# Delta rule in two groups of steps, six ticks apart, with two projections between the products of the last step

## The chip, the core and the metric

The program runs on one core of a Trainium2 chip. Times are device microseconds of one execution; lower is better. In the profile PE is TensorE's matmuls and PEld its weight loads, DVE is VectorE, ACT is ScalarE, POOL is GpSimd, and SP is SyncE, which only starts transfers. The text calls VectorE "Vector".

## What is computed

The reference runs two blocks of a network on 256 tokens of width 1024, in float32. The first has attention, a gated recurrence, a dense MLP and a mixture of 8 experts. The second has a linear attention in two forms, the gated delta rule and HGRN2, each run in both directions over 256 context and 256 latent tokens, then a mixture of 32 experts. This case is about the delta rule and what stands right behind it. The reference computes, for each direction, chunk by chunk of tokens:

```python
a = jnp.where(strict, jnp.einsum('nbhik,nbhjk->nbhij', kb, k) * decay, 0.0)
rhs = jnp.concatenate([v * beta[..., None], kb * jnp.exp(gcum)[..., None]], axis=-1)
sol = lax.linalg.triangular_solve(a, rhs, left_side=True, lower=True, unit_diagonal=True)
u, w = sol[..., :dv], sol[..., dv:]

def step(s, inp):
    qc, kc, uc, wc, gc, dc = inp
    v_new = uc - jnp.einsum('bhck,bhkv->bhcv', wc, s)
    g_last = gc[..., -1]
    s_new = s * jnp.exp(g_last)[..., None, None] + jnp.einsum(
        'bhck,bhcv->bhkv', kc * jnp.exp(g_last[..., None] - gc)[..., None], v_new)
    ...
    o = jnp.einsum('bhck,bhkv->bhcv', qc * jnp.exp(gc)[..., None], s) + jnp.einsum(
        'bhij,bhjv->bhiv', jnp.einsum('bhik,bhjk->bhij', qc, kc) * dc, v_new)
    return s_new, o
```

Only the state `s` goes from one chunk to the next. The triangular solve and all of `a` belong to one chunk alone.

## The kernel before

Everything is laid out by hand: five instruction streams, one per engine, that meet only in semaphores. Each engine works through its stream in order. `pe.wait_ge(*at("gram", n))` waits until the n-th event of that name has been counted.

**The delta rule.** The tokens are cut into four chunks of 128, two of context, two of latent tokens; `TILE` gives the order for each direction `d`. The loop `for s_ in range(4)` stands once in each of the four compute streams. One step does both directions, four heads each, so most operations are four matmuls of 128x128, or one vector operation of 128x512. Its phases are:

1. Gram (L1037, L1039): `k k^T` and the cumulated gates, in steps 2 and 3 also `k q^T` (L1043). Vector and ScalarE form decays from it (L1673 to L1677, L1884).
2. Start: Vector forms `A` (L1683), masks it and subtracts it from the identity, which gives `T` (L1690, L1691); in steps 2 and 3 it also masks `attT` (L1687, L1688). TensorE transposes `A` (L1051), ScalarE copies it to `At`, and Vector forms `U` from that (L1695, L1696).
3. Six levels that invert the triangle by doubling. GpSimd masks `At` for each level (L2204). TensorE multiplies that with `T` (L1066, the product), ScalarE copies the result to `P1`, TensorE multiplies `P1` with `U` in two ways (L1073 for T, L1075 for U, the level step), and Vector subtracts both from `T` and `U` (L1702, L1703). The sixth level has no T.
4. Key: GpSimd scales `v` and `k` by the gates (L2210, L2212, L2216; L2215 for q), TensorE multiplies the key by `U` (L1083), and ScalarE copies it as `nw`.
5. Value: the new value from `U`, `vb`, `nw` and the state `Sd` (L601), which Vector copies as `vn` (L1706).
6. State: in steps 2 and 3 the output (L601), and the addition to the state (L1103), which Vector adds in (L1720, L1721; event `S_ready`).

The steps do not overlap: the gram product of a step waits for `S_ready` of the step before. All eight PSUM banks serve one step, four per direction, and its nine work buffers per direction, `WK[d]`, lie in the arena:

```python
WK = [[area(8192 + 4608 * d + 512 * i, H, P) for i in range(9)] for d in range(2)]
...
if s_:
    pe.wait_ge(*at("S_ready", n - 1))
```

**Behind it** stand two projections of the second linear attention, `zd` and `hq` (helper line L601, four chains of eight products each, 64 matmuls in the trace), a sum of squares between them (L1114, event `o_ss`), ScalarE's Ln and Exp of it (`rs_done`), the SiLU of hq (`hq_ready`), then the projections `f0` and `hi`. `f0` waits for `hq_ready`.

**The weights.** A ring of six slots of 2 MB holds weights; SP loads them in the order of a list (`plan`, `plan2`: k, v, q, zd, hq, f0, hi, f1, hz, gd0, gd1, gh0, gh1, ...), each when the slot's former user has been read. `READ` names that event, and SP's queue is in order.

**The start of the kernel.** TensorE waits for 19 small rows, transposes them to columns (L832, L833), and then transposes the normed input (`norm_T(0)`, L632). On ScalarE `norm(0)` stands behind the exponentials for lambda and the SiLU of c; on Vector it stands behind the same work (L1437 to L1447).

The functions that the change touches, with the lines of the profile:

## Time and profile before

| What | us |
|---|---|
| Median of 3 runs | 2853.5 (2852.21 to 2855.32) |
| The profiled execution | 2852.58 |
| Its span, first to last instruction | 2850.8 |
| TensorE busy in the span | 2497.5 (88%) |
| Vector busy | 630.4 (22%) |
| ScalarE busy | 369.2 (13%) |
| GpSimd busy | 151.4 (5%) |
| Delta rule, first gram to last state product | 1652.1 to 1941.9 |
| First f0 matmul | 1978.1 |

The span is what lies between the first and the last instruction of the profiled execution; the time of a run is 1.8 us longer. In time by stretch each line gives a stretch, its length, the busy time of each engine with the number of instructions, the granted TensorE clock as a share of full speed, and the share and rate of the transfers. A float32 matmul shows as two instructions, so that four of 128x128 are "x8". Busy times of TensorE overlap a little, since matmuls are pipelined; what a group costs is read from one start to the next, or from the chain.

### The profile page before, as it was taken

The numbers are of one execution on the slowest core, as the hardware profiler recorded it, in microseconds if no ns is written. First come the engines' busy times: TensorE is split into PE (matmuls) and PEld (weight loads), VectorE is DVE, ScalarE is ACT, GpSimd is POOL, SyncE is SP. The second block draws the span as 40 slices with busy tenths as digits, with TensorE's granted clock in tenths as the row PEclk, the third lists the DMA queues.
The fourth block names the chain that finished last, engine by engine and source line by source line (L and its number), as shares of the span: only waits on it lengthen the run. The fifth ranks groups of instructions, "written<-read, shape, count | busy, mean of one in ns | idle before, by whom it ended". The sixth has DMA issues, their size and how long they took to land.

```text
span 2850.8 us, 52823 instructions
## 1 busy us (share of the span) xinstructions
PE 2497.5 (88%) x24386; PEld 1612.6 (57%) x24386; DVE 630.4 (22%) x1191; ACT 369.2 (13%) x595; POOL 151.4 (5%) x140
## 2 busy tenths in 40 slices
PE   5768997699999999999998967678898959999896
PEld 4536775556656555655656667676467634444343
DVE  1441001300000000000002344551534142222223
ACT  1021001100000000000001221111323011011101
POOL 1000000000000000000000023321201000000000
PEclk9879999799999999999999988888999979999998
DMA  7484333399989989998996200001111249999994
GB/s 280 148 296 147 120 133 126 125 393 353 393 312 352 394 309 393 352 394 315 353 393 228 89 1 1 1 1 60 59 60 59 89 177 399 404 397 398 401 401 186
DMA packets 273245, 676.25 MB, mean 237 GB/s; under 512 B 5876, under 2 KB 9423, under 8 KB 268815
## 3 DMA queue, kind: packets, MB, share of 16 engines
q1 hardware_dynamic: 270608, 666.91, 62.3%
q0 software_dynamic: 2112, 6.04, 0.6%
q8 instruction: 184, 3.01, 0.4%
q14 instruction: 23, 0.18, 0.0%
q10 hardware_dynamic: 318, 0.10, 0.0%
HBM read 671.98 MB, written 1.05 MB: 236 GB/s over the span
## 4 chain that ended last, share of the span: by engine, by line
PE 59%; DMA 10%; DVE 5%; ACT 3%; POOL 3%; issue 2%; SPq 2%; DVEq 0%; POOLq 0%; ACTq 0%
PE ps L691 21%; PE ps L601 14%; PE ps L712 10%; DMA ring<-in_w_exp_up 10%; PE ps L776 5%; ACT arena L1884 2%; SPq L548 2%; PE ps L1075 1%; PE ps L1073 1%; PE ps L1066 1%; PE ps L698 1%; PE ps L674 1%; POOL arena L2236 1%; ACT L1884 1%; POOL arena L2204 1%
## 5 line engine op out<-in xcount | busy, mean ns | idle before, releaser
L691 PE MATMUL ps<-ring,arena 128*32 128x256 f32 x10752 | 598.0, 382 | 16.6 <-issue 15.3
L691 PEld LDWEIGHTS ps<-ring,arena 128*32 128x32 f32 x10752 | 349.0, 111 | 249.6 <-issue 32.0
L601 PE MATMUL ps<-hT,ring 128*128 128x256 f32 (+1 forms) x1792 | 444.2, 409 | 19.6 <-ACT arena L1884 7.3
L1884 ACT ACTIVATE arena<-ps 128x512 f32<-128x512 f32 (+4 forms) x347 | 186.8, 556 | 1960.7 <-PE ps L691 576.1
L601 PEld LDWEIGHTS ps<-hT,ring 128*128 128x128 f32 x1792 | 346.9, 194 | 122.6 <-issue 69.4
L712 PE MATMUL ps<-ring,arena 128*32 128x256 f32 x5376 | 300.5, 379 | 0.0
L776 PE MATMUL ps<-ring,arena 128*64 128x512 f32 x1024 | 233.8, 611 | 29.4 <-DMA ring<-in_w_exp_up 26.5
L712 PEld LDWEIGHTS ps<-ring,arena 128*32 128x32 f32 x5376 | 173.9, 110 | 115.3 <-issue 1.3
L1359 DVE TENSOR_TENSOR arena<-arena,ps 128x384 f32<-128x384 f32 x56 | 31.0, 554 | 825.2 <-ACT arena L1884 825.2
L776 PEld LDWEIGHTS ps<-ring,arena 128*64 128x64 f32 x1024 | 81.1, 141 | 178.9 <-issue 178.9
L601 PE MATMUL ps<-arena 128*128 128x128 f32 (+1 forms) x1144 | 146.1, 290 | 20.6 <-DVE arena L1387 7.5
L601 PEld LDWEIGHTS ps<-arena 128*128 128x128 f32 x1144 | 142.8, 206 | 22.5 <-DVE arena L1387 7.7
L2204 POOL TENSOR_TENSOR arena<-arena,table 128x512 f32<-128x512 f32 x48 | 65.3, 1367 | 1533.6 <-ACT arena L1884 1476.3
L792 PE MATMUL ps<-ring,arena 128*64 128x512 f32 x512 | 113.4, 595 | 0.0
L1884 ACT ACT_TABLE_LOAD x64 | 82.1, 1283 | 193.1 <-PE ps L601 87.0
L1066 PE MATMUL ps<-arena 128*128 128x128 f32 x384 | 59.4, 305 | 34.0 <-POOL arena L2204 20.7
L1884 ACT ACTIVATE arena<-arena 128x512 f32<-128x512 f32 (+3 forms) x78 | 63.1, 845 | 186.9 <-DVE arena L1677 41.1
L941 PE MATMUL ps<-ring,arena 128*128 128x512 f32 x176 | 79.0, 592 | 0.0
L1410 DVE TENSOR_TENSOR arena<-arena,ps 128x512 f32<-128x512 f32 x16 | 11.0, 687 | 300.0 <-PE ps L776 300.0
L1066 PEld LDWEIGHTS ps<-arena 128*128 128x128 f32 x384 | 52.9, 214 | 39.2 <-POOL arena L2204 22.5
L792 PEld LDWEIGHTS ps<-ring,arena 128*64 128x64 f32 x512 | 35.3, 137 | 66.6 <-issue 66.6
L601 PE MATMUL ps<-ring,arena 128*128 128x512 f32 (+1 forms) x160 | 58.1, 524 | 12.3 <-DVE arena L1265 9.7
(319 smaller groups left out, 1721.5 us busy)
## 6 DMA issues: line engine op xcount, KB each, us to landing
ring<-in_moe_wg SPq DMA_DIRECT2D x56, 2048.0 KB, 11.3
ring<-in_moe_wu SPq DMA_DIRECT2D x56, 2048.0 KB, 16.4
ring<-in_moe_wd SPq DMA_DIRECT2D x56, 2048.0 KB, 17.2
ring<-in_w_exp_gate SPq DMA_DIRECT2D x32, 2048.0 KB, 17.5
ring<-in_w_exp_up SPq DMA_DIRECT2D x32, 2048.0 KB, 18.8
ring<-in_w_exp_down SPq DMA_DIRECT2D x32, 2048.0 KB, 14.8
ring<-in_w_in SPq DMA_DIRECT2D x13, 2048.0 KB, 8.9
ring<-in_w_ada SPq DMA_DIRECT2D x12, 2048.0 KB, 8.1
```

Source lines behind the costliest of these rows:

```text
L548: sp.dma_start(dst, w[2 * p + j, :, :].rearrange(rows_, p=P))\
L601: last = mm(outp, l, r, start=(i == 0), stop=(i == n - 1))
L674: last = mm(ps[:, 4 + q, t * S:(t + 1) * S], un_GcT[32 * q:32 * q + 32, 1 - b, 3 * t + r, :], ysb[32 * q:32 * q + 32, r * S:(r + 1) * S], ...
L691: last = mm(flat[32 * q:32 * q + 32, S * r:S * r + S], x_[:, k, 32 * r:32 * r + 32], gu[:, :, k, q * P:(q + 1) * P], start=(k == 0), stop= ...
L712: last = mm(flat[32 * q:32 * q + 32, 3 * 512 + S * r:3 * 512 + S * r + S], un_actT[:, c, r, :], d_[:, c, q * S:(q + 1) * S], start=(j == 0 ...
L776: last = mm(ps[64 * j:64 * j + 64, part, :], x_[:, k, 64 * j:64 * j + 64], weights(3 * j + part, KC)[:, k, :], start=(k == 0), stop=(k == ...
L792: last = mm(ps[64 * j:64 * j + 64, 4 + h_, :], pr_actT[:, c, 64 * j:64 * j + 64], weights(3 * j + 2, 4)[:, c, h_ * 512:(h_ + 1) * 512], st ...
L941: last = mm(ps[:, 4 + 2 * t + c, :], actb[:, (n - 1) % 4, t * P:(t + 1) * P], d_[:, j, c * 512:(c + 1) * 512], start=(n == 1), stop=(n == ...
L1066: last = mm(ps[:, 4 * d + 1, h * P:(h + 1) * P], Ao[:, h, :], T[:, h, :], start=True, stop=True)
L1359: V.tensor_tensor(un_act, un_sg, up_, ALU.mult).then_inc(inc("m1_act"), 1)
L1884: return nc.scalar.activation(*a, **k)
L2204: G.tensor_tensor(WK[d][2 + l % 2], WK[d][1], rep(level_mask(l, d == 0), 4), ALU.mult)\
```

## The change

It has three parts.

1. The steps of the delta rule are put into two groups, even and odd. Time is counted in 30 ticks; step `s_` starts in tick 6 `s_` (`FIRST`) and has twelve phases, one per tick: gram, turn, start of U, six levels, key, value, state. So from tick 6 to tick 23 each tick holds one level of one step and another phase of the other. Each stream has a loop over ticks. TensorE does the level products, then the other phase, then the level steps. Each group has four PSUM banks, two per direction, its own work buffers and its own semaphores for T, U, P and the masks; a product now waits for T alone. The buffers of group 1 lie in ring slots 0 to 2, so the slots of k, v and q are only given back with the last `S_ready`. `k q^T` moves from gram to key. GpSimd's scalings are spread over the levels.
2. `zd` and `hq` are computed in ticks 27 to 29, chain by chain between the products of step 3. The sum of squares moves to banks 4 and 5, hq to 2 and 3; `f0` waits for `rs_done` and `hi` for `hq_ready`.
3. At the start of the kernel `norm(0)` comes first on ScalarE and Vector, and `norm_T(0)` comes before the transposes of the rows.

```diff
-        READ = {"k": ("k_proj", 4), "v": ("v2_proj", 4), "q": ("q_proj", 1), "zd": ("zd_proj", 1), "hq": ("hq_proj", 1),
+        READ = {"k": ("S_ready", 8), "v": ("S_ready", 8), "q": ("S_ready", 8), "zd": ("zd_proj", 1), "hq": ("hq_proj", 1),
...
-        WK = [[area(8192 + 4608 * d + 512 * i, H, P) for i in range(9)] for d in range(2)]
+        spare = ring[:, 0:3, :].rearrange("p s n -> p (s n)")
+
+        def work(g, o):
+            return area(8192 + o, H, P) if g == 0 else spare[:, o:o + 512].rearrange("p (a b) -> p a b", a=H)
+
+        WK = [[[work(g, 4608 * d + 512 * i) for i in range(9)] for d in range(2)] for g in range(2)]
...
+        FIRST = (0, 6, 12, 18)
+        GRAM, INV, HALF, UPDATE, KEY, VALUE, STATE = 0, 1, 2, 8, 9, 10, 11
+
+        def in_tick(k):
+            return [(s_, k - FIRST[s_]) for s_ in range(4) if GRAM <= k - FIRST[s_] <= STATE]
+
+        def levels(k):
+            return [(s_, p - HALF) for s_, p in in_tick(k) if HALF < p <= UPDATE]
```

TensorE's stream, with the helpers that wait:

```diff
+            def turn(s_, d):
+                n = 2 * s_ + d
+                A, (bx, by) = WK[s_ % 2][d][0], banks(s_, d)
+                pe.wait_ge(*at("A_ready", n + 1))
+                pe.wait_ge(*at("eR", n + 1))
...
+            def product(s_, d, l):
+                g = s_ % 2
+                Ao, T, (bx, by) = WK[g][d][2 + l % 2], WK[g][d][4], banks(s_, d)
+                pe.wait_ge(*at("Aoff%d_ready" % g, level_count(s_, d, l)))
+                pe.wait_ge(*at("T%d_ready" % g, t_count(s_, d, l - 1)))
+                if l == 1:
+                    pe.wait_ge(*at("U%d_ready" % g, u_count(s_, d, 0)))
...
+            def step(s_, d, l):
...
+                pe.wait_ge(*at("P%d_copied" % g, level_count(s_, d, l)))
+                pe.wait_ge(*at("U%d_ready" % g, u_count(s_, d, l - 1)))
...
+            for k in range(FIRST[3] + STATE + 1):
+                for s_, l in levels(k):
                     for d in range(2):
...
+                        product(s_, d, l)
+                for s_, p in in_tick(k):
                     for d in range(2):
...
+                        if p == GRAM:
+                            gram(s_, d)
+                        elif p == KEY:
+                            key(s_, d)
+                        elif p == VALUE:
+                            value(s_, d)
+                        elif p == STATE:
+                            state(s_, d)
+                if k == FIRST[3] + KEY:
+                    pe.wait_ge(*at("S_ready", 6))
+                    for m in range(3):
+                        project("zd", m, 0)
+                elif k == FIRST[3] + VALUE:
+                    project("zd", 3, 0)
+                    for m in range(2):
+                        project("hq", m, 2)
+                elif k == FIRST[3] + STATE:
+                    for m in range(2, 4):
+                        project("hq", m, 2)
+                for s_, l in levels(k):
+                    for d in range(2):
+                        step(s_, d, l)
+                for s_, p in in_tick(k):
+                    if p == INV:
+                        for d in range(2):
+                            turn(s_, d)
...
-                    pe.wait_ge(*at("hq_ready", 1))
+                    pe.wait_ge(*at("rs_done", 1))
```

Vector's loop and GpSimd's (ScalarE's has the copies of P1 first, then gram, turn or key):

```diff
+            for k in range(FIRST[3] + STATE + 1):
+                for s_, p in in_tick(k):
+                    for d in range(2):
+                        if p == GRAM:
+                            gram(s_, d)
+                        elif p == INV:
+                            start_T(s_, d)
+                        elif p == HALF:
+                            start_U(s_, d)
+                        elif p == KEY and s_ >= 2:
+                            attend(s_, d)
+                        elif p == VALUE:
+                            value(s_, d)
+                        elif p == STATE:
+                            state(s_, d)
+                for s_, l in levels(k):
+                    for d in range(2):
+                        step(s_, d, l)
...
+                        if l <= 4:
+                            offs(s_, d, l + 2)
+                for s_, p in in_tick(k):
+                    for l in (1, 2):
+                        for d in range(2):
+                            if p == HALF:
+                                offs(s_, d, l)
+                    for d in range(2):
+                        if p == HALF + 1:
+                            key_decayed(s_, d)
+                        elif p == HALF + 5:
+                            key_to_end(s_, d)
+                        elif p == HALF + 6:
+                            value_scaled(s_, d)
```

The start, on TensorE and on ScalarE:

```diff
             pe.wait_ge(*at("table_in", 16))
+            norm_T(0)
             pe.wait_ge(*at("rows_in", 16 * (len(ROWS_A) + len(ROWS_B))))
...
-
-            norm_T(0)
...
+            norm(0, res, ("x_in", 16))
             ac.wait_ge(*at("cols_ready", 1))
...
-            norm(0, res, ("x_in", 16))
```

TensorE at the end of the levels of step 0, before the change (L1066 product, L1075 the U product, L1083 key):

```order
L1066 MATMUL ps<-arena 128x128 [waits TU_ready,Aoff_ready]
L1066 MATMUL ps<-arena 128x128 x3
L1066 MATMUL ps<-arena 128x128 [waits TU_ready,Aoff_ready]
L1066 MATMUL ps<-arena 128x128 x3
L1075 MATMUL ps<-arena 128x128 [waits P1_copied]
L1075 MATMUL ps<-arena 128x128 x3
L1075 MATMUL ps<-arena 128x128 [waits P1_copied]
L1075 MATMUL ps<-arena 128x128 x3
L1083 MATMUL ps<-arena 128x128 [waits kbg_ready,TU_ready]
L1083 MATMUL ps<-arena 128x128 x3
L1083 MATMUL ps<-arena 128x128 [waits kbg_ready,TU_ready]
L1083 MATMUL ps<-arena 128x128 x3
```

The same place after the change (L1086 the U product, L1074 product, L1095 key; names with 0 and 1 belong to the groups):

```order
L1086 MATMUL ps<-arena 128x128 [waits U0_ready,P0_copied]
L1086 MATMUL ps<-arena 128x128 x3
L1086 MATMUL ps<-arena 128x128 [waits U0_ready,P0_copied]
L1086 MATMUL ps<-arena 128x128 x3
L1074 MATMUL ps<-ring 128x128 [waits U1_ready,T1_ready,Aoff1_ready]
L1074 MATMUL ps<-ring 128x128 x3
L1074 MATMUL ps<-ring 128x128 [waits U1_ready,T1_ready,Aoff1_ready]
L1074 MATMUL ps<-ring 128x128 x3
L1095 MATMUL ps<-arena 128x128 [waits ops_ready,U0_ready]
L1095 MATMUL ps<-arena 128x128 x3
L1095 MATMUL ps<-arena 128x128 [waits ops_ready,U0_ready]
L1095 MATMUL ps<-arena 128x128 x3
```

The first level product of step 1, in the ring's buffers, now stands between the last level step of step 0 and its key product. Before, it stood behind key, value and state of step 0 and gram and turn of step 1.

ScalarE at the start of the kernel, before (rows of `pA`, `pB`, `rowsA` and `rowsB` are lambda, the gates and c; `res` is the input):

```order
L1884 ACT_TABLE_LOAD [waits ve_mixer1]
L1884 ACTIVATE small<-small 128x2 [waits ve_mixer1]
L1884 ACTIVATE small<-pA 128x4 [waits ac_mixer1]
L1884 ACTIVATE small<-small 128x4 [waits ac_step]
L1884 ACT_TABLE_LOAD
L1884 ACTIVATE small<-small 128x4 [waits ac_step]
L1884 ACT_TABLE_LOAD [waits scT_zero]
L1884 ACTIVATE rowsA<-pB 128x4 [waits ac_mixer1]
L1884 ACTIVATE rowsA<-pB 128x4
L1884 ACTIVATE rowsB<-pB 128x4 x2
L1884 ACTIVATE arena,small<-res 128x1024 [waits x_in,ac_mixer1]
L1884 ACTIVATE arena,small<-res 128x1024
```

After:

```order
L1964 ACT_TABLE_LOAD
L1964 ACTIVATE arena,small<-res 128x1024 [waits x_in]
L1964 ACTIVATE arena,small<-res 128x1024
L1964 ACT_TABLE_LOAD [waits ms_ready]
L1964 ACTIVATE small<-small 128x2 [waits sumsq]
L1964 ACT_TABLE_LOAD
L1964 ACTIVATE small<-small 128x2 [waits ac_step]
L1964 ACTIVATE small<-small 128x2 [waits ve_mixer1,rstd_ready]
L1964 ACTIVATE small<-pA 128x4 [waits ac_mixer1]
L1964 ACTIVATE small<-small 128x4 [waits ac_step]
L1964 ACT_TABLE_LOAD
L1964 ACTIVATE small<-small 128x4 [waits ac_step]
```

The squares of the input moved from behind that work to the head, behind a table load that waits for nothing.

## Rows read from the trace of the kernel before

**Rows 1.** Time by stretch: busy us (count) of each engine, granted clock, DMA
```profile
core 0: us, PE busy (x) PEld busy (x) DVE busy (x) ACT busy (x) POOL busy (x), PEclk, DMA share, GB/s
1652.10:1719.00 66.90, 50.61 (x361) 47.91 (x361) 29.94 (x47) 12.33 (x24) 22.16 (x18) 0.83 0.00 1
...
1863.60:1941.90 78.30, 55.94 (x425) 53.67 (x423) 36.91 (x58) 13.37 (x26) 25.01 (x20) 0.83 0.00 1
1669.20:1677.60 8.40, 8.03 (x48) 7.76 (x49) 3.57 (x4) 1.19 (x2) 3.63 (x3) 0.67 0.00 0
1669.20:1707.20 38.00, 34.40 (x272) 33.22 (x272) 15.82 (x23) 7.16 (x12) 12.05 (x10) 0.93 0.00 1
```
**Rows 2.** In order of time (start us, us, what): one level; its chain
```profile
1679.32 1.13 PE L1066 MATMUL ps<-arena 128*128 128x128 f32 x8 [0.65 <-DVE arena L1703]
...
1682.35 0.69 DVE L1702 TENSOR_TENSOR arena<-arena,ps 128x512 f32<-128x512 f32 x1 [3.17 <-PE ps L1075]
...
1685.57 1.13 PE L1066 MATMUL ps<-arena 128*128 128x128 f32 x8 [0.65 <-DVE arena L1703]
...
1680.45 0.89 PE ps L1073 x8
```
**Rows 3.** In order of time, opening of step 0; in brackets idle before and releaser
```profile
1652.14 2.08 PE L1037 MATMUL ps<-arena 128*128 128x128 f32 x8 [6.25 <-DVE arena L1662]
...
1659.94 1.12 DVE L1683 SCALAR_TENSOR_TENSOR arena<-ps,small,arena 128x128 f32<-128x128 f32 x4
...
1661.10 0.69 DVE L1690 TENSOR_TENSOR arena<-arena,table 128x512 f32<-128x512 f32 x1
...
1669.20 2.05 PE L1066 MATMUL ps<-arena 128*128 128x128 f32 x8 [4.35 <-POOL arena L2204]
```
**Rows 4.** The same after the last level of step 0; then clock by stretch there
```profile
1709.58 1.13 PE L1083 MATMUL ps<-arena 128*128 128x128 f32 x8 [2.26 <-POOL arena L2216]
...
1712.00:1714.00 2.00, 1.30 (x6) 1.33 (x7) 0.00 (x0) 0.00 (x0) 0.56 (x1) 0.56 0.00 0
1714.00:1716.00 2.00, 2.00 (x13) 2.00 (x13) 0.00 (x0) 0.60 (x1) 0.00 (x0) 0.59 0.00 0
```
**Rows 5.** In order of time, end of delta rule to f0; clock of its start
```profile
1961.43 13.98 PE L601 MATMUL ps<-hT,ring 128*128 128x256 f32 x64
...
1966.02 1.06 ACT L1884 ACTIVATE arena<-arena 128x1024 f32<-128x1024 f32 x1
...
1978.13 1.71 PE L601 MATMUL ps<-hT,ring 128*128 128x512 f32 x2 [2.72 <-ACT arena L1884]
...
1978.00:1980.00 2.00, 1.87 (x3) 0.97 (x4) 0.00 (x0) 0.00 (x0) 0.00 (x0) 0.62 1.05 409
```
**Rows 6.** Loads, KB each, us to landing; waits of TensorE for DMA, whole span
```profile
ring<-in_w_in SPq DMA_DIRECT2D x13, 2048.0 KB, 8.9
...
table<-in_k_table POOLq DMA_DIRECT2D x1, 1216.0 KB, 12.5
res<-in_x POOLq DMA_DIRECT2D x1, 1024.0 KB, 9.4
...
PE ps L776 <- DMA ring<-in_w_exp_up: 26.5, 14, 2.6
```
**Rows 7.** In order of time, the opening of the kernel
```profile
24.91 1.06 ACT L1884 ACTIVATE arena<-res 128x1024 f32<-128x1024 f32 x1
...
32.04 3.68 PE L632 MATMUL ps<-table,arena 128*128 128x128 f32 x16 [13.93 <-DVE arena L1265]
...
36.50 27.89 PE L601 MATMUL ps<-hT,ring 128*128 128x256 f32 x128 [0.78 <-DVE hT L1271]
```
**Rows 8.** In order of time, Vector beside GpSimd in step 1 and later
```profile
1729.88 6.45 POOL L2204 TENSOR_TENSOR arena<-arena,table 128x512 f32<-128x512 f32 x4 [1.72 <-ACT arena L1884]
1730.19 1.63 DVE L1696 TENSOR_TENSOR arena<-table,arena 128x512 f32<-128x512 f32 x1
...
2052.14 1.33 DVE L1779 COPY_PREDICATED arena<-table,ps 128x512 f32<-128x512 int32 x2
```

More of the change, by code:

```diff
@@ L1107, in _ @@
             pe.wait_ge(*at("S_ready", 8))
[L1108 to L1111 removed]
             pe.wait_ge(*at("o_sq", 1))
             for i in range(2):
[L1114 removed]
+                last = mm(ps[:, 4 + i, :], ones, rs[:, 2 * i:2 * i + 2, :], start=True, stop=True)
```

394 lines of the change are left out of this document (200 added, 194 removed).

## The prediction

> **What bounds the kernel now.** I read the page first, then time by stretch, then the chain and the instructions in order of time of one stretch, then the waits at its two ends. The profiled execution took 2852.6 us (span 2850.8), 0.9 us under the median of the three runs, 2853.5; the sum below is made against 2852.6. TensorE is busy 88% of the span and leads the chain; expert weights end the last 500 us. Neither is touched. The change sits in two places: the first 36.5 us, and the delta rule with the two projections behind it.
>
> The delta rule runs from 1652.1 to 1941.9 in four steps, the first of 66.9 and the last of 78.3 us, and TensorE is busy only 51 and 56 us of these, at a granted clock of 0.83 [rows 1]. Inside a step one level takes 6.25 us (1679.32 to 1685.57): two products and the T and U products of both directions are six groups of four matmuls (x8 in the rows) at 0.89 us, so 5.4 us of work, and 0.65 us go in waiting for the second of Vector's subtractions [rows 2]. So the levels are nearly full; the loss is around them. Step 0 needs 17.06 us from its first gram product to the first level product (1652.14 to 1669.20) [rows 2, 3], its six levels 38.0 us [rows 1], and the rest of the 66.9 is the tail, in which TensorE waits for GpSimd's scaled operands (2.26 us before the first key product) and then runs at 0.56 to 0.59 of the clock until 1716 [rows 4]. Outside the levels a step thus costs 66.9 - 38.0 = 28.9 us, and 78.3 - 38.0 = 40.3 us in the last two, which also form an output.
>
> **The change, part by part.** Call u the time of four matmuls of 128x128 at full clock, 0.89 us [rows 2]. The new order has 30 ticks. In ticks 6 to 23 one step is in its levels 4 to 6, key, value and state, while the next one is in gram, turn, start and levels 1 to 3. The order of the matmuls is in the listings: between the level products and the level steps of one group now stands a phase of the other.
>
> (1) Opening of step 0 to its first level product: unchanged, 17.1 us. (2) Levels 1 to 3 of step 0 alone: the first as now, 8.4 us (1669.2 to 1677.6, at a clock of 0.67 [rows 1]); the other two lose the 0.65 us wait, since a product now waits for T only, not for T and U: 5.6 us each. Sum 19.6.
>
> (3) Ticks 6 to 23, counted in u. By tick of a group of six: level 4 with gram 6 + 4; level 5 with turn 6 + 1; level 6 has no T product, 4; level 1 with key 6 + 2; level 2 with value 6 + 4; level 3 with state 6 + 2. That is 47u when step 1 is the older one; 45u when it is step 0 (its value has no old state, 2u less); 53u when it is step 2 (kq +2, output +4). Together 145u = 129.1 us. To this come waits that the order leaves. In the tick with turn, Vector has 2 x (1.12 + 0.69 + 0.69) = 5.0 us of start-T before 2.75 us of level subtractions (four at 0.69) [rows 2, 3], against 6.2 us of TensorE work: about 1.6 us late. In the next tick TensorE has 4u = 3.6 us, but the first product of the younger step needs the At copy, GpSimd's two masks and Vector's start-U; TensorE waited 4.35 us there [rows 3], and more for the second direction, which comes 2.4 us later. Against 3.6 us of cover I take 2.9 us late. So 4.5 us per group, 13.5 in all. After such a gap the clock falls: after the wait before 1709.58 the stretch 1712 to 1716 got 0.56 to 0.59 [rows 4], which costs about 2 us; three gaps, 6 us. Sum (3): 148.6 us, 8.3 us per tick.
>
> (4) Ticks 24 to 29, step 3's last levels, key, value, state: 6 + 6 + 4 + 4 + 4 + 6 = 30u = 26.7 us, with 0.6 us of waits left, and six of the eight projection chains between them. Both projections have 64 matmuls; at 13.98 us for one [rows 5] a chain costs 3.5 us, six cost 21.0. The copies of nw and vn and the masks of attT (0.6 to 1.4 us each) hide beneath them; without that cover each would show. Sum 48.3.
>
> (5) From the last state product to the first f0 product. Now: 1941.9 to 1978.1, 36.2 us [rows 5]. After: two chains (7.0 us) cover Vector's last S (about 2.4 us after the product) and ScalarE's square; then o_ss 1.9 us, Ln and Exp 1.1 each with a table load of 1.3 between: 12.5 us with handovers [rows 5]. f0 now waits for that Exp (rs_done) and no longer for the SiLU of hq, which moves beneath f0's 29.4 us. The idle of 3.6 us before f0 replaces one of 2.7 us, after which f0 already began at 0.62 of the clock [rows 5]: no difference.
>
> Sum: 17.1 + 19.6 + 148.6 + 48.3 + 12.5 = 246.1 us against 1978.1 - 1652.1 = 326.0. Gain 79.9.
>
> (6) The ring. Group 1 works in slots 0 to 2, so hi, f1 and hz, loaded behind the k, v and q projections so far, are asked for only after the last S, and on SP's queue gd0, gd1 and gh0 stand behind them. A 2 MB load of w_in lands in 8.9 us [rows 6]; hi is first needed about 10 + 29.4 us after the last S, f1 much later. Cost 0, hidden under f0; without f0 in its slot hi would cost up to 8.9 us.
>
> (7) The start. The norm stood on ScalarE behind lam and the c gates: its square began at 24.91, the first projection at 36.50 [rows 7]. The input lands 9.4 us after its issue at 1.3, so at 10.7, the table 12.5 us after 2.1 [rows 6]. Squares, Ln, Exp and the scaling take 24.91 to 32.04, 7.1 us: 17.8 [rows 7]. The 19 small rows are in at 17.5, where the transposes of rows stand now. Sixteen transposes 3.7, the two transposes of rows 0.55, Vector's four ops 0.6, four hT copies 2.9, which no longer run beneath the transposes, and 0.5 of handovers: 26.0. Gain 10.5; the 3.9 us without TensorE before the projection cost about 2 of it, by what the clock does behind such gaps [rows 4, 5]. Gain 8.5. The weights of win0 were issued at 0.74 and are no later than the table. ScalarE's lam and c work moves beneath the first projection (27.9 us); until then nothing waits for it. Of the waits of TensorE for loads the large one is that for w_exp_up in the last stage, 26.5 us in 14 [rows 6]; nothing before it hangs on a weight, so the shift should be kept.
>
> Total gain 79.9 + 8.5 = 88.4, and 2852.6 - 88.4 = **2764 us**. Bounds: with no waits and no clock losses (13.5 + 6 + 2 less) 2743; with the lock below in full 2795.
>
> **The lock between Vector and GpSimd.** A Vector operation with both inputs in SBUF took 0.69 us alone [rows 3] and 1.63 us while four of GpSimd's masks ran, 1.61 us each; two COPY_PREDICATED with one input in PSUM took 1.33 together beside a GpSimd operation [rows 8]. The level subtractions read one operand from PSUM, so I take 0.68 for them beside GpSimd too. The Trainium skill (SBUF — State Buffer, Who interferes with whom) says that Vector with two SBUF inputs and a GpSimd operation that reads SBUF exclude each other for a whole instruction, and that one SBUF input is free of it; the trace agrees, 1.63 against 0.66. By that rule the start, gram, attT and S operations, which now meet the masks of the other group, would all pay, and the sum would be the first rival's.
>
> **Rivals.** *The lock bounds the ticks.* Some 15.5 locked Vector operations per step (gram 2 to 4, start-T 4, start-U 4, attT 2, S 2, rounded), each 0.94 us longer: 14.6 us per step. If they all lie on the path in the three groups, 43.8 us in place of my 13.5: 2764 + 30.3 = 2795. For it: both queues are in order, and Vector does the other group's phase before the level's subtractions. Against: GpSimd is busy only 22 us of 67 and 25 of 78 per step [rows 1], and level ticks have 2.5 us of it.
> *The ticks run in series.* If the phases overlap nothing, a tick costs 6.25 plus a sixth of 28.9 to 40.3, mean 5.8: 18 x 12.0 = 216 us in place of 148.6: 2831. For it: one semaphore waited for in a wrong place holds a whole in-order queue. Against: products and steps of a level are independent of the phase between them.
> *Slower.* Series and full lock together: 216 + 43.8 in place of 148.6, so 2875. It decides in ticks 6 to 23, where all other parts sum to 97.5, from a tick of (326.0 + 8.5 - 97.5) / 18 = 13.2 us on; I expect 8.3.
> *The start gives nothing*, because something other than the norm holds the first projection: 2773.
>
> **Chances.** Forecast 0.77, lock 0.14, series 0.05, slower 0.02, no gain at the start 0.02. The range is 2740 to 2798: forecast with its bounds, the lock, and the start without gain; outside stay series and slower. 0.2% is 5.7 us, about what a measurement of this kernel tells from no change. Faster by more 0.97, within 0.01, slower 0.02.
>
> **What would show it.** First projection at about 26 us. Delta rule from its first gram to f0 in 246 us, the clock in it above 0.93 instead of 0.84, level ticks of 7 to 10 us, and TensorE's waits at the first product of steps 1 to 3 near 3 us. Locked: Vector's start operations at 1.6 us mean. Series: TensorE busy 50 of 70 us as now. hi loads begin after the last S and no matmul waits for them. I am wrong if a double tick averages over 10 us or if the second half does not simply move earlier.

## The result, and the profile after

The changed kernel took 2768.4 us, median of four runs (2762.65 to 2773.21), beside 2853.3 us of the kernel before on the same chip: a ratio of 0.970, with a 95% interval of 0.968 to 0.972. Five more runs later gave a median of 2764.0 (2762.19 to 2769.42). The prediction was 2764. The profiled execution took 2765.3 us, span 2763.4.

From the first gram product to the first f0 matmul, "the stretch" from here on, TensorE now needs 244.2 us in place of 326.0. Time by stretch in the changed kernel, first the opening with levels 1 to 3 of step 0, then the first and the last of the three groups of six ticks, and the whole:

```profile
core 0: us, PE busy (x) PEld busy (x) DVE busy (x) ACT busy (x) POOL busy (x), PEclk, DMA share, GB/s
1643.69:1680.28 36.59, 27.86 (x184) 26.35 (x185) 19.99 (x32) 7.32 (x16) 15.41 (x12) 0.74 0.00 0
1680.28:1725.06 44.78, 42.04 (x362) 40.78 (x361) 30.15 (x48) 11.99 (x24) 21.68 (x18) 1.00 0.01 1
...
1772.27:1825.79 53.52, 49.37 (x427) 48.01 (x425) 38.60 (x59) 12.99 (x26) 25.07 (x20) 1.00 0.01 1
1643.69:1887.90 244.21, 220.11 (x1717) 209.81 (x1717) 137.53 (x215) 58.10 (x107) 98.02 (x84) 0.96 0.05 17
```

And the whole stretch in the kernel before:

```profile
1652.14:1978.13 325.99, 244.02 (x1716) 229.11 (x1717) 139.24 (x221) 62.20 (x113) 99.08 (x84) 0.85 0.03 8
```

TensorE's busy time fell from 244.0 to 220.1 us, for the same matmuls (1716 and 1717 records) at a granted clock of 0.96 in place of 0.85, and what is not busy fell from 82.0 to 24.1 us. So of 81.8 us, 57.9 are idle time that went and 23.9 are clock. In [rows 1] one step of 66.9 us had 51 us of work at 0.83; now six ticks of 44.8 us hold 42.0 at 1.00.

TensorE's largest waits in the stretch for Vector (us in total, times, longest):

```profile
PE ps L1074 <- DVE arena L1747: 6.9, 3, 4.3
...
PE ps L1063 <- DVE arena L1736: 4.0, 2, 2.5
PE ps L1074 <- DVE ring L1747: 3.5, 3, 2.2
PE ps L1074 <- DVE arena L1754: 3.2, 3, 1.4
PE ps L1074 <- DVE ring L1754: 1.2, 1, 1.2
```

L1063, where the turn waits for A, is left only in the opening. L1747 is the end of start-U, L1754 the T subtraction; together 14.8 us, of which 10.1 lie in ticks 6 to 23 and the rest in the opening, the successor of [rows 3]. The wait of [rows 4] for GpSimd's scaled operands is gone. The same waits in the kernel before, over its stretch, in the order A at the turn, masks at the first product, scaled operands at the key, T or U at a product:

```profile
PE ps L1051 <- DVE arena L1683: 22.5, 8, 4.3
PE ps L1066 <- POOL arena L2204: 20.7, 5, 6.1
PE ps L1083 <- POOL arena L2216: 20.0, 8, 3.5
PE ps L1066 <- DVE arena L1703: 12.9, 20, 0.6
```

The tick from 1742.0, in order of time, in which the older step is in level 6 and the younger in start-U. TensorE, then Vector, then GpSimd:

```profile
1742.01 2.32 PE L1074 MATMUL ps<-ring 128*128 128x128 f32 x16 [1.18 <-DVE ring L1754]
...
1746.08 1.13 PE L1074 MATMUL ps<-arena 128*128 128x128 f32 x8
1749.43 1.13 PE L1074 MATMUL ps<-arena 128*128 128x128 f32 x8 [2.22 <-DVE arena L1747]
...
1743.58 0.68 DVE L1746 TENSOR_TENSOR arena<-arena,table 128x512 f32<-128x512 f32 x1
1744.29 1.65 DVE L1747 TENSOR_TENSOR arena<-table,arena 128x512 f32<-128x512 f32 x1
1745.86 1.76 DVE L1746 TENSOR_TENSOR arena<-arena,table 128x512 f32<-128x512 f32 x1
1747.65 1.64 DVE L1747 TENSOR_TENSOR arena<-table,arena 128x512 f32<-128x512 f32 x1
...
1741.10 5.97 POOL L2300 TENSOR_TENSOR arena<-arena,table 128x512 f32<-128x512 f32 x4 [3.60 <-ACT arena L1964]
```

The product at 1749.43 waits 2.22 us for U of the second direction. Vector's four operations take 0.68, 1.65, 1.76 and 1.64 us, and GpSimd's four masks run from 1741.10 to 1747.07 beside them, with a fifth from 1747.29 on. Grouped by shape, start-U of group 0 and, for comparison, the T subtraction that reads PSUM:

```profile
L1754 DVE TENSOR_TENSOR arena<-arena,ps 128x512 f32<-128x512 f32 x20 | 13.7, 685 | 17.6 <-PE ps L1086 17.5
...
L1746 DVE TENSOR_TENSOR arena<-arena,table 128x512 f32<-128x512 f32 x4 | 5.8, 1461 | 0.1
...
L1747 DVE TENSOR_TENSOR arena<-table,arena 128x512 f32<-128x512 f32 x4 | 5.6, 1401 | 0.1
```

The end of the stretch, TensorE and then ScalarE's two table loads. The two hq chains of the last tick end, and TensorE waits 5.0 us for Ln and Exp; compare [rows 5]:

```profile
1874.11 7.07 PE L615 MATMUL ps<-hT,ring 128*128 128x256 f32 x32
1881.02 1.88 PE L1171 MATMUL ps<-arena,table 128*128 128x512 f32 x4
1887.90 2.73 PE L615 MATMUL ps<-hT,ring 128*128 128x512 f32 x3 [5.00 <-ACT arena L1964]
...
1882.98 1.28 ACT L1964 ACT_TABLE_LOAD   x1 [3.17 <-PE ps L1171]
...
1885.40 1.28 ACT L1964 ACT_TABLE_LOAD   x1
```

The start, compare [rows 7]; the first projection begins 11.6 us earlier, and the first gram product comes at 1643.69 in place of 1652.14:

```profile
18.09 3.34 PE L646 MATMUL ps<-table,arena 128*128 128x128 f32 x16 [18.09 <-DVE arena L1317]
...
24.91 7.30 PE L615 MATMUL ps<-hT,ring 128*128 128x256 f32 x26 [3.31 <-DVE hT L1323]
```

### The profile page after: what moved, and what is told of

Same layout as the page of the kernel before. It is cut to its first block, busy times and chain, and to the rows that moved or that the text cites. A ratio compares the mean times of both kernels' runs of the same rounds, so it can differ in the third digit from the quotient of the medians.

```text
span 2763.4 us, 52753 instructions
## 1 busy us (share of the span) xinstructions
PE 2475.1 (90%) x24386; PEld 1594.1 (58%) x24386; DVE 631.6 (23%) x1191; ACT 369.1 (13%) x596; POOL 150.4 (5%) x140
## 3 DMA queue, kind: packets, MB, share of 16 engines
HBM read 671.98 MB, written 1.05 MB: 244 GB/s over the span
## 4 chain that ended last, share of the span: by engine, by line
PE 59%; DMA 10%; DVE 5%; ACT 3%; issue 2%; SPq 2%; POOL 1%; DVEq 0%; ACTq 0%
PE ps L705 21%; PE ps L615 14%; PE ps L726 11%; DMA ring<-in_w_exp_up 10%; PE ps L790 5%; ACT arena L1964 2%; SPq L562 2%; PE ps L1074 1%; PE ps L1086 1%; PE ps L1084 1%; PE ps L712 1%; PE ps L688 1%; POOL arena L2356 1%; ACT L1964 1%; PE ps L806 1%
## 5 line engine op out<-in xcount | busy, mean ns | idle before, releaser
L1964 ACT ACTIVATE arena<-ps 128x384 f32<-128x384 f32 (+5 forms) x311 | 165.2, 552 | 1825.9 <-PE ps L705 576.2
L615 PE MATMUL ps<-arena 128*128 128x128 f32 (+1 forms) x1048 | 132.4, 287 | 20.6 <-DVE arena L1439 7.5
L615 PEld LDWEIGHTS ps<-arena 128*128 128x128 f32 x1048 | 128.7, 204 | 22.5 <-DVE arena L1439 7.6
L2300 POOL TENSOR_TENSOR arena<-arena,table 128x512 f32<-128x512 f32 x24 | 32.1, 1356 | 1441.9 <-ACT arena L1964 1415.2
L615 PE MATMUL ps<-ring,arena 128*128 128x512 f32 (+2 forms) x176 | 61.2, 502 | 12.3 <-DVE arena L1317 9.7
L646 PE MATMUL ps<-table,arena 128*128 128x128 f32 x96 | 19.7, 391 | 57.1 <-DVE arena L1317 57.1
L777 PE MATMUL ps<-arena 128*128 128x512 f32 x136 | 62.9, 605 | 1.1 <-ACT arena L1964 1.1
## 6 DMA issues: line engine op xcount, KB each, us to landing
ring<-in_moe_wd SPq DMA_DIRECT2D x56, 2048.0 KB, 17.2
```

Source lines behind the costliest of these rows:

```text
L615: last = mm(outp, l, r, start=(i == 0), stop=(i == n - 1))
L777: last = mm(ps[:, (6 if t == 0 else 4) + c, :], GcT[:, 1 - b, t, :], ysb[:, c * 512:(c + 1) * 512], start=True, stop=True)
L1964: return nc.scalar.activation(*a, **k)
L2300: G.tensor_tensor(WK[g][d][2 + l % 2], WK[g][d][1], rep(level_mask(l, d == 0), 4), ALU.mult)\
```

## The experiments

Nothing of the computation is left out in any of them. Since every trace has its own start, I compare the stretch, first gram product to f0. It came out as 244.21 and 244.23 us in two profiled executions of the changed kernel, whose whole times were 2765.3 and 2762.2; whole times of one kernel differ from run to run by up to 12 us. Each stretch below is that of one profiled execution. Rows marked with one run have no second one, so their stretch is used and not their time.

| kernel | stretch, us | time, us (runs) |
|---|---|---|
| before | 326.0 | 2853.3 (4) |
| start alone | 326.0 | 2847.0 (11) |
| changed | 244.2 | 2768.4 (4), 2764.0 (5) |
| projections behind | 244.4 | 2766.4 (5) |
| product waits for T and U | 256.9 | 2778.7 (5) |
| twelve ticks apart | 272.0 | 2793.4 (5) |
| twelve ticks apart, late scalings | 299.0 | 2817.7 (1) |
| late scalings | 267.3 | 2789.0 (1) |
| masks later | 234.8 | 2752.9 (1) |
| start-U reads PSUM | 235.5 | 2756.9 (1) |
| tail order | 239.2 | 2764.7 (1) |
| better | 229.3 | 2744.0 (5) |
| better, start-T split | 239.8 | 2754.4 (4) |

**The start alone.** The kernel before, with part 3 of the diff and nothing else.

> The kernel before with part 3 of the change alone (the norm first at the start). My term (7): the first projection starts at about 25 us instead of 36.5, 8.5 us of it are left at the delta rule's first gram product (1643.7), and the time is 2844.8 us, 8.5 under the kernel before. Rival, the start gives nothing because the weights or the tables hold what follows: 2853. Second rival, the gain is spent in the second half, where transfers bound the expert stage: between 2848 and 2853.

Measured 2847.0 us (2845.7 to 2855.9), ratio 0.9986 with an interval of 0.9977 to 0.9995; the first gram product at 1644.92. By the medians (2853.7 beside it for the kernel before) that is 6.7 us of the expected 8.5; by the ratio, into which the longer runs go too, it is 4.0 (1.4 to 6.6). From f0 to the end it needs 873.0 us, the kernel before 872.7, so nothing is spent in the second half, and the second rival falls. Eight of the eleven runs lie at 2845.7 to 2848.9 and three at 2853.2 to 2855.9, where nothing is gained. None of these three was profiled; the next experiment's trace shows such a loss in another kernel.

**The projections behind the delta rule.** Part 2 undone:

```diff
-                if k == FIRST[3] + KEY:
-                    pe.wait_ge(*at("S_ready", 6))
-                    for m in range(3):
-                        project("zd", m, 0)
...
             pe.wait_ge(*at("S_ready", 8))
+            for m in range(4):
+                project("zd", m, 0)
...
             last.then_inc(inc("o_ss"), 1)
+            for m in range(4):
+                project("hq", m, 2)
...
-                    pe.wait_ge(*at("rs_done", 1))
+                    pe.wait_ge(*at("hq_ready", 1))
```

> The changed kernel with part 2 undone: zd and hq stand behind the last S again, with the sum of squares between them, and f0 waits for the SiLU of hq. Theory: ticks 24 to 29 lose the six chains (21 us) and show some 8 us of copies that those covered, so 35 us in place of 48.3; from the last state product to f0 36 us as in the kernel before, in place of 13.8. Net 9 us longer than the changed kernel: 2777 us. Rival, the chains hid nothing and only the 5 us behind o_ss are saved by the order: 2773 or less. Rival, the chains hide all waits of the tail: 2782 or more.

Measured 2766.4 us, no longer than the changed kernel, and a stretch of 244.4. The time from tick 24 to f0 is 62.3 us here and 62.1 there. In order of time, zd, hq and f0:

```profile
1865.78 14.08 PE L615 MATMUL ps<-hT,ring 128*128 128x256 f32 x64 [2.16 <-DVE arena L1775]
...
1881.42 13.98 PE L615 MATMUL ps<-hT,ring 128*128 128x256 f32 x64
...
1898.12 2.85 PE L615 MATMUL ps<-hT,ring 128*128 128x512 f32 x3 [2.72 <-ACT arena L1957]
```

The last product of the step ends at 1863.6, 27.8 us after tick 24 began, where pure work is 26.7: without the chains between them the products of step 3 wait for nothing, since while Vector or ScalarE copies one direction TensorE has the other's work. The 21 us of chains had covered nothing. Behind the last product, Vector's last S shows with 2.16 us, because zd waits for it; then hq covers Ln and Exp, and 2.72 us of SiLU show. That is 4.9 us in place of the 5.0 of the changed kernel, so the new order behind the sum of squares saved nothing either. The rival "they hid nothing" holds.

This profiled execution took 2773.0 us, its first gram product came at 1653.74, 10 us later than in the changed kernel's, over the same code. The 10 us are in TensorE's busy time, not in its waits: from the first projection to the first gram product it is busy 1499.9 us here and 1489.3 there. The same 32 matmuls, first in the changed kernel, then here:

```profile
479.18 7.17 PE L615 MATMUL ps<-ring,arena 128*128 128x256 f32 x32 [2.64 <-DVE arena L1618]
```

```profile
482.25 10.23 PE L615 MATMUL ps<-ring,arena 128*128 128x256 f32 x32 [2.65 <-DVE arena L1611]
```

7.17 us against 10.23, at a granted clock of 1.00 against 0.68, and in the projections that follow (513.0 to 536.2 in the one, 519.2 to 545.5 in the other) it was 0.63 against 0.55. So what differs between these two executions is where the clock falls around the waits; 9.3 of the 10 us were there by 546 us. The trace of the tail order below is of the same kind: 10.22 us for these matmuls, and its first gram product at 1652.22.

**Product waits for T and U.** One line in `product`:

```diff
-                if l == 1:
-                    pe.wait_ge(*at("U%d_ready" % g, u_count(s_, d, 0)))
+                pe.wait_ge(*at("U%d_ready" % g, u_count(s_, d, l - 1)))
```

> The changed kernel with the product of every level waiting for U beside T, as the kernel before did. Nothing else differs. Theory, the products follow the level steps directly in the new order too, so 0.65 us come back in each of 20 level products, less the ticks in which the turn lies between: 11 us longer than the changed kernel, 2779 us. Rival, in the ticks with two phases Vector is ahead and the wait costs nothing there: only the five ticks of a group alone pay, 3 us, 2771.

Measured 2778.7 us, and 12.7 us more in the stretch. The waits for Vector's subtractions rose from 4.4 to 14.0 us:

```profile
PE ps L1073 <- DVE arena L1754: 7.8, 11, 1.6
...
PE ps L1073 <- DVE ring L1754: 6.2, 10, 1.3
```

Idle time rose by 9.0 us (to 33.1) and busy time by 3.7 (to 223.8), at a clock of 0.95. The theory holds: the order of phases does not hide this wait, since products follow the level steps directly.

**Twelve ticks apart.** `FIRST = (0, 12, 24, 36)`, so that steps never overlap.

> The changed kernel with its steps twelve ticks apart in place of six, so that no phase of one step lies beside another's; everything else as changed (T-only wait, earlier scalings, projections between the last products). Theory, the overlap is the gain of ticks 6 to 23: of the 290 us of four steps some 28 go by the T-only wait (13), the earlier scalings (9) and the gram that no longer waits for S (7), 13 net come in by the chains, 13.8 stand behind: 289 us from first gram to f0 in place of 244, so 2813 us. Rival, most of the gain comes from the finer waits and not from the overlap: under 2790. Rival, these waits give nothing alone: 2831 or more.

Measured 2793.4 us, where I expected 2813; the stretch:

```profile
1645.45:1917.43 271.98, 232.18 (x1717) 220.04 (x1717) 134.07 (x215) 58.56 (x107) 99.25 (x84) 0.89 0.04 15
```

Overlap gives 27.8 us of the 81.8, and 54 come without it. Neither my figure for this run nor the rival's 2831 in the prediction had that right; the rival "under 2790" was missed by 3 us, but what it says, that most of the gain needs no overlap, is so. What the 54 are is asked by the next two.

**Late scalings**, once twelve and once six ticks apart. GpSimd's stream:

```diff
-                        if p == HALF + 1:
-                            key_decayed(s_, d)
-                        elif p == HALF + 5:
-                            key_to_end(s_, d)
-                        elif p == HALF + 6:
-                            value_scaled(s_, d)
+                        if p == HALF + 6:
+                            po.wait_ge(*at("TU%d_step" % (s_ % 2), level_count(s_, d, 6)))
+                            key_to_end(s_, d)
+                            key_decayed(s_, d)
+                            value_scaled(s_, d)
```

> The kernel with steps twelve ticks apart, and GpSimd's scalings late as above. Theory, that kernel's stretch from first gram product to f0 (272.0 us against 326.0 before) was short for the most part because the scalings had been moved ahead of the key products: with them late about 20 us of waits and 4 to 6 us of lower clock come back, 296 to 298 us. Rival, the gain without overlap comes from the T-only wait and the separate buffers: 280 or less.

Measured in the stretch 299.0 us against 272.0:

```profile
1643.88:1942.84 298.96, 243.26 (x1716) 229.62 (x1717) 134.12 (x215) 58.48 (x107) 99.29 (x84) 0.86 0.04 14
```

The key products wait 15.8 us (8.5 and 7.3 for the two groups), and TensorE's busy time rose by 11.1 us, from 232.2 to 243.3, with the clock at 0.86 in place of 0.89. So 27 of the 54 us without overlap come from moving the scalings ahead of the key product.

The traces of the four kernels also say where the rest lies. TensorE's time in the stretch, us:

| TensorE waits for | before | twelve ticks, late scalings | twelve ticks | changed |
|---|---|---|---|---|
| A, at the turn | 22.5 | 17.6 | 17.6 | 4.0 |
| masks or start-U, at the first product | 20.7 | 17.3 | 17.2 | 10.4 |
| scaled operands, at the key | 20.0 | 15.8 | 0 | 0 |
| T or U, at a later product | 12.9 | 0 | 0 | 4.4 |
| last S, f0 and short waits | 5.9 | 5.0 | 5.0 | 5.3 |
| idle in all | 82.0 | 55.7 | 39.8 | 24.1 |
| busy | 244.0 | 243.3 | 232.2 | 220.1 |

Without overlap and with late scalings 27.0 us are gained over the kernel before: 12.9 are the waits of a product for T and U, 8.3 shorter waits at turn and first product, 4.2 a shorter wait for the scalings, which are thus not placed exactly as before, and the rest small. The overlap then takes 13.6 us from the turn and 6.8 from the first product, brings 4.4 for T, and takes 12.1 from the busy time.

> The changed kernel with GpSimd's scalings of k, v and q all behind the last level step of their step, as in the kernel before (there the key products waited 20.0 us for them in all), on GpSimd's queue behind the masks of the younger step. Theory, with another step's products on TensorE in front of the key products the late scalings are nearly hidden: 1 to 2 us for each of the three groups and 3 us at the last step, 250 us from first gram product to f0 in place of 244.2. Rival, the in-order queue holds TensorE as before: 262 or more. Rival, they cost nothing: 245 or less.

Measured 267.3 us, where I expected 250. Waits for GpSimd, three rows in order of time from the second group, and the stretch:

```profile
PE ps L1095 <- POOL ring L2319: 6.7, 4, 3.5
...
PE ps L1095 <- POOL arena L2319: 5.1, 4, 2.0
...
1753.14 1.13 PE L1074 MATMUL ps<-arena 128*128 128x128 f32 x8 [0.39 <-DVE arena L1747]
1756.27 1.30 PE L1074 MATMUL ps<-arena 128*128 128x128 f32 x8 [2.00 <-DVE arena L1747]
1758.17 2.04 PE L1095 MATMUL ps<-ring 128*128 128x128 f32 x8 [0.60 <-POOL ring L2319]
...
1645.80:1913.05 267.25, 232.61 (x1717) 220.62 (x1717) 134.49 (x215) 58.26 (x107) 100.05 (x84) 0.91 0.04 15
```

The waits for the scalings are 11.8 us here and were 15.8 without overlap, so the overlap hides some of them, less than I expected. But the stretch grew by 23.0 us: 10.5 are idle and 12.5 are matmuls that got longer, at a clock of 0.91 in place of 0.96. After gaps of 0.4, 2.0 and 0.6 us the key product of four matmuls (x8) took 2.04 us, where it takes 1.06 at full clock; the granted clock from 1757 to 1763 was 0.51, about the lower of its two levels (1.2 of 2.4 GHz). One microsecond of waiting cost about two here; where a product waits for T and U it cost 1.4 (9.0 idle, 3.7 busy). The size is that of the rival (262 or more), by a mechanism that it did not name.

**Masks later.** GpSimd's masks of level 2 wait until U stands:

```diff
                             if p == HALF:
+                                if l == 2:
+                                    po.wait_ge(*at("U%d_ready" % (s_ % 2), u_count(s_, 1, 0)))
                                 offs(s_, d, l)
```

> The changed kernel with GpSimd's two masks of level 2 held back until Vector has finished both U of the step; nothing leaves, only the time of two GpSimd operations moves. The stretch from the first gram product to f0 took 244.2 us in the changed kernel. Theory, Vector's start-U (1.4 us mean against 0.69 alone) is held by GpSimd's masks and by nothing else, and is what the second product of level 1 waits for: Vector's start-U falls below 1.0 us mean, the three waits of 0.9, 2.2 and 2.2 us before that product go, the opening of step 0 loses 1 to 2 us, and the stretch is 237.5 us. Rival, the wait comes from the copy of the turned matrix and the queue order, not from the lock: 243 to 245. Rival, the later masks of level 2 are now waited for: over 246.

Measured 234.8 us, 9.4 less than the changed kernel. The waits for start-U fell from 10.4 to 3.4 us, all of it in the opening, and the operations stand as follows:

```profile
PE ps L1074 <- DVE arena L1747: 3.4, 1, 3.4
...
L1746 DVE TENSOR_TENSOR arena<-arena,table 128x512 f32<-128x512 f32 x4 | 3.8, 952 | 0.1
...
L1747 DVE TENSOR_TENSOR arena<-table,arena 128x512 f32<-128x512 f32 x4 | 2.8, 693 | 0.1
```

The mask operation is down from 1.46 to 0.95 us and the subtraction from 1.40 to 0.69; in group 1 both stand at 0.69. That is nearly what they take alone. Nothing but the time of two GpSimd operations per step was moved, and two more semaphore waits were added, so it is shown that GpSimd's masks held start-U, the lock of the prediction, and that this was on the path. The busy time fell too, by 2.4 us (220.1 to 217.7).

**Start-U reads PSUM.** Vector's first operation takes the turned matrix from its bank, the wait for ScalarE's copy stays:

```diff
-                At, U, tmp = WK[g][d][1], WK[g][d][5], WK[g][d][6]
+                At, U, tmp = banks(s_, d)[1], WK[g][d][5], WK[g][d][6]
```

> The changed kernel with Vector's first operation of start-U reading the turned matrix from PSUM in place of ScalarE's copy of it (the wait for the copy stays, so nothing starts earlier). Theory, an operation with one input in PSUM is not held by GpSimd: that operation takes 0.69 us instead of 1.4 to 1.6, the other stays as it is, and the stretch from first gram product to f0 is 238 to 240 us in place of 244.2. Rival, the lock is about any use of SBUF by both engines: no operation gets shorter, 244.

Measured 235.5 us, less than the 238 to 240 that I expected. The operation with one input in PSUM takes 0.68 us while the same masks run beside it (in one tick at 1742.04, beside masks from 1740.30 to 1743.26). The second one fell as well, to 1.0 us on the mean, which I had not expected; in that tick both of its operations (1.11 and 1.05 us) still ran beside masks. Why they waited less than a whole mask is not shown:

```profile
L1747 DVE TENSOR_TENSOR arena<-table,arena 128x512 f32<-128x512 f32 x4 | 4.1, 1027 | 0.1
...
L1746 DVE TENSOR_TENSOR arena<-ps,table 128x512 f32<-128x512 f32 x4 | 2.7, 686 | 0.1
```

**Tail order.** The chains behind the products again, in the order that covers most: zd without a wait for the last S, the sum of squares, hq, and `f0` waiting for `rs_done`.

```diff
-            pe.wait_ge(*at("S_ready", 8))
+            pe.wait_ge(*at("S_ready", 6))
+            for m in range(4):
+                project("zd", m, 0)
+            pe.wait_ge(*at("S_ready", 8))
             pe.wait_ge(*at("o_sq", 1))
...
             last.then_inc(inc("o_ss"), 1)
+            for m in range(4):
+                project("hq", m, 2)
```

> The changed kernel with the tail edit alone: zd as one block directly behind the last product of step 3, without a wait for the last S, then the sum of squares, then hq as one block, f0 waiting for rs_done and hi for hq_ready. The start and all masks as in the changed kernel. Theory: placed between the products the chains cover nothing, since the copies there are covered by the other direction anyway; placed behind, zd covers the last S and hq covers Ln and Exp. From the last state product's end to f0 13.98 + 1.7 + 13.9 us, so the stretch from first gram product to f0 is 239.3 us in place of 244.2. Rival, the copies of ticks 27 to 29 show without the chains: 242 or more.

Measured 239.2 us, as expected; from the last product to f0 TensorE has no wait left. This trace had its first gram product at 1652.22, so its whole time, 2764.7, shows nothing of the gain.

**Better.** The three edits above, and the two transposes of the rows ahead of `norm_T(0)` again.

> The changed kernel with four edits: both of the two above; zd as one block behind the last product of step 3 without a wait for the last S, then the sum of squares, then hq as one block over ScalarE's Ln and Exp, f0 waiting for rs_done; and at the start the transposes of the rows again before those of the normed input. Expected in the stretch from first gram product to f0: 8 us less by the two masks edits, 4.9 less by the tail (the wait of 2.2 for the last S and of 2.7 for the SiLU of hq are gone, and the 5.0 us behind the sum of squares are filled), 244.2 to 231.3. The first projection starts at 23 us instead of 24.9. Time 2754 us against 2768 of the changed kernel. Rival, the tail edit gives nothing, as the chains between the products gave nothing: 236 in the stretch.

Measured 2744.0 us (2742.8 to 2755.1), and 229.3 in the stretch where I expected 231.3; ratio to the kernel before 0.9635 (0.9618 to 0.9653), while the changed kernel beside it on the same chip had 0.9696 (0.9683 to 0.9709). The first projection starts at 22.67. Of the 14.9 us less in the stretch 5.0 are the tail; the two edits at start-U, 9.4 and 8.7 alone, give about 10 together, since they take away the same wait. Between the profiled executions of the two kernels on this chip, 18.4 us apart, the stretch is 15.0, the time ahead of it 1.6 and the time behind it 1.8.

```profile
1641.93:1871.20 229.27, 217.88 (x1716) 208.97 (x1717) 130.46 (x221) 58.30 (x108) 95.11 (x84) 0.97 0.11 38
```

What is left of TensorE's waits in the groups is the T subtraction (L1748 here), 4.4 us; in the opening 2.7 us for start-U are left.

**The changed kernel again.** Nothing is edited.

> The changed kernel again, beside the one above on one chip. Expected 2768 us with single runs from 2762 to 2774, since what varies lies ahead of the delta rule; the stretch from first gram product to f0 again 244.2 us within 0.3. Rival, the spread is in the delta rule: the stretch differs by over 1 us.

Measured 2764.0 us (2762.2 to 2769.4); the stretch 244.23. The spread lies outside the delta rule.

**Start-T split.** In the better version Vector does `A`, then the other step's subtractions, and only then mask and subtraction of T.

```diff
                 done(last, "A_ready")
+
+            def finish_T(s_, d):
...
                 for s_, l in levels(k):
                     for d in range(2):
                         step(s_, d, l)
+                for s_, p in in_tick(k):
+                    if p == INV:
+                        for d in range(2):
+                            finish_T(s_, d)
```

> The better version (229 us from first gram product to f0) with Vector's start-T cut in two: A first, then the other step's level subtractions, then mask and subtraction for T. Theory, what is left of the waits in the two ticks of turn and start-U (4.4 us for T's subtraction) is Vector's sum of work over both ticks, so order moves it and does not remove it: 228 to 231 us. Rival, only the order was wrong: 4.4 us less, 225. Rival, the work now falls under GpSimd's masks and is locked: 232 or more.

Measured 239.8 us in the stretch and 2754.4 in all, 10.5 worse. The moved operations now start when GpSimd's masks do:

```profile
1740.64 1.73 DVE L1737 TENSOR_TENSOR arena<-arena,table 128x512 f32<-128x512 f32 x1
1742.40 1.65 DVE L1738 TENSOR_TENSOR arena<-table,arena 128x512 f32<-128x512 f32 x1
...
PE ps L1074 <- DVE arena L1745: 8.2, 2, 5.2
PE ps L1074 <- DVE ring L1745: 6.7, 4, 3.2
```

These two took 1.73 and 1.65 us; on the mean of both directions and groups the pair takes 1.20 and 1.17 in place of 0.97 and 0.69. Behind them on the queue start-U is late: 14.9 us of waits where the better version has 2.7. The wait for T's subtraction that the edit was after did go, from 4.4 to 0.6. The size is that of the last rival (232 or more), and the lock that it names is there. But it is not all: in this tick it adds 2.0 us, while the four moved operations put 2.7 us of their own in front of start-U. No run takes the two apart.

## Why the prediction was right, and where it was not

The time was right, 2764 forecast against 2768.4 and 2764.0, and so was the sum of the stretch, 246.1 against 244.2. In part that is luck: in (3) three errors of 3 to 6 us cancel for the most part, and two thirds of the gain need no overlap, which my rival of ticks in series did not allow for. By its own steps:

- (1) opening: 17.1 forecast, 17.0 measured. (2) levels 1 to 3: 19.6 and 19.6. The wait for T alone is worth 12.7 us in the stretch by its undoing.
- (3) ticks 6 to 23: 148.6 forecast, 145.5 measured. 145u are 129.1 us, as counted; the other 16.4 are 10.1 of waits, where I had 13.5, and 6.3 of handovers between groups of matmuls, for which I had nothing (two level products, 2u or 1.78 us, take 2.00 from start to start). Of the waits, those for T's subtraction came out at 4.4 us (4.8 forecast) and those for start-U at 5.7 (8.7 forecast). The 6 us for clock losses are wrong: the clock stayed at 1.00 in all three groups. I had taken the price from [rows 4] for gaps of 2.9 us; the gaps came out at 0.3 to 2.2. With more of them close together it does fall, as late scalings show.
- The cause that I gave for the 2.9 us in the tick of level 6 was wrong. I put them down to the chain of copy, masks and start-U without the lock; masks later shows that without the lock they are gone, and the wait behind start-U in the opening falls from 4.3 to 3.4 us. My main case excluded the lock from the path and the first rival laid all of it there, 43.8 us; at start-U it is worth 9.4. Other operations with two SBUF inputs stay longer than the 0.69 us of one alone, for example 0.95 us on the mean for the masking of T (L1739) and 1.02 for that of attT (L1761). That this is the lock too is likely, but no run took it away, so its price is open. The Trainium skill (SBUF — State Buffer, Who interferes with whom) says that a Vector instruction with two SBUF inputs contends with a GpSimd instruction that reads SBUF, and one with at most one SBUF input, outside the two-port modes, does not. These runs agree: 1.65 to 1.76 us in the one case, 0.68 with the other input in PSUM.
- (4) 48.3 forecast, 48.3 measured, and (5) 12.5 against 13.8, but the step "hide beneath them; without that cover each would show" failed: undoing the placement left the stretch as it was. The two terms were right as a sum of work, and that sum could be had with the projections where they stood. (5) was also 1.3 us short, because the table for Ln is loaded only after the sum of squares is there.
- (6) ring: no matmul waits for hi, f1 or hz in the trace. No run changed the slots, so a price without f0's cover stays open.
- (7) start: first projection at 26.0 forecast, 24.9 measured, and 8.45 us left at the first gram product against 8.5. Alone it gave 6.7 by the medians of eleven and fifteen runs, and 4.0 by the ratio.
- Behind f0 the profiled execution lost 2.8 us (875.5 us to the end, against 872.7 before). The repeated changed kernel needed 872.6, so that is no effect of the change.

The rivals: the series case was priced at 2831 and measures 2793. It took the 28.9 to 40.3 us around the levels as fixed by the missing overlap, while two thirds of the gain do not need it: of 81.8 us, 27.0 are the scalings moved ahead and 27.8 the overlap (taken in that order; in the other order the overlap comes first, 299.0 to 267.3, with 31.7, and the scalings give 23.0). Of the remaining 27.0 the traces put 12.9 at the products, which no longer wait for T and U, and 8.3 at turn and first product. The tail has no part in it, since undoing it changed 0.2 us. What shortened the waits at turn and first product no run takes apart.

## What to carry to other kernels

When independent steps are interleaved, count each tick in the bounding engine's work; here the count gave 129.1 of 145.5 us, and the rest was waits and handovers. Check in traces which part of a gain needs the interleaving: here 54 of 81.8 us did not. Then look at which operations of two other engines start together in the tick: here two GpSimd operations per step, moved by a few microseconds, were worth 9.4 us. Before filling supposed waits with other work, look whether the work of the other direction or stage fills them already, and put the filler where the trace shows a wait, behind a sum of squares rather than between products. Compare such changes over a stretch between two fixed instructions when the rest of the program varies by more than the effect.

## What the runs showed of the hardware

- A wait inside dense work can cost its length again in clock: late scalings added 10.5 us of idle time and 12.5 us of longer matmuls, while in the changed kernel gaps of up to 2.2 us left the granted clock at 1.00 in all three groups. The price is not fixed: 9.0 us of idle time brought 3.7 where products wait for T and U.
- The stretch repeats within 0.02 us in two executions, while identical code before it varied by 10 us, in which the granted clock had part (7.17 against 10.23 us for the same 32 matmuls, at 1.00 against 0.68). With the new start alone 8 of 11 runs had its gain and three did not. Why the clock at these gaps varies more behind the new start than in the kernel before (2851.0 to 2857.0 over 15 runs) is open.
- GpSimd pays for the lock as well, though less: its masks took 1.34 to 1.36 us on the mean in the changed kernel, where they meet start-U, and 1.28 in masks later, where they do not.
